# Moving the halves of x by 32 bytes, and adding a three-pass product at the old place

## The reference

```python
def first_block(x, ...):
    for i in range(2):
        h = rmsnorm(x, mix_norm[i])
        x = x + (pool_mixer(h, ...) if i == 0 else chunk_attention(h, ...))
        h = rmsnorm(x, ffn_norm[i])
        x = x + conv_ffn(h, ffn_w_gate[i], ffn_w_val[i], ...)     # D_FF = 2816
    return x

def conv_ffn(h, w_gate, w_val, conv_w, conv_b, w_out):
    a = h @ w_gate                       # then a causal convolution over 3 tokens
    return (jax.nn.silu(a) * (h @ w_val)) @ w_out

def second_block(x, ...):
    proj = rmsnorm_2(x, norm_attn) @ w_in
    # retention, group norm, silu gate            -> y_a = ret @ w_branch_ret
    # stick-breaking attention                    -> y_b = sb @ w_branch_sb
    x = x + (sigmoid(ga) * y_a + sigmoid(gb) * y_b) @ w_out
    x = x + peer(rmsnorm_2(x, norm_ffn), ...)      # 16384 experts, top 16 per head
    return x
```

## Time and profile before

| | |
|---|---|
| Median of 3 runs | 1524.32 us (1523.0 to 1524.53) |
| The profiled execution, its own time | 1520.35 us |
| Its span, from the first instruction to the last | 1518.5 us |
| Instructions | 26337 |
| TensorE matmuls, busy | 1488.9 us, 98% of the span |
| VectorE, ScalarE, GpSimd busy | 1107.8, 764.5, 328.1 us |
| Granted TensorE clock | full, in all 40 slices |
| Read from HBM | 341.92 MB, 226 GB/s over the span |

### The profile page before, as it was taken

How to read it: one execution, slowest core, us unless ns; L and a number is a source line. 1 busy time by engine, 2 the same in 40 slices (tenths; PEclk the granted TensorE clock), 3 DMA queues, 4 the chain that set the end, 5 groups by cost and what they waited for, 6 DMA issues and landing times.

```text
span 1518.5 us, 26337 instructions
## 1 busy us (share of the span) xinstructions
PE 1488.9 (98%) x10162; PEld 1374.1 (90%) x10162; DVE 1107.8 (73%) x2153; ACT 764.5 (50%) x1562; POOL 328.1 (22%) x240
## 2 busy tenths in 40 slices
PE   6999999999999999999999999999999999999998
PEld 6999997799999988899999999999999977777777
DVE  6766678767666776766768895677777688888887
ACT  7555555555555556444454113443343366666665
POOL 1111113202111121001016001233232223332330
PEclk9999999999999999999999999999999999999999
DMA  5666556445656564444544577999999889888885
GB/s 186 190 193 189 189 196 212 132 140 166 186 191 193 170 204 161 144 139 138 172 154 140 169 241 260 335 316 351 322 312 326 320 308 314 302 303 311 307 311 185
DMA packets 95852, 344.68 MB, mean 227 GB/s; under 512 B 10665, under 2 KB 11953, under 8 KB 95729
## 3 DMA queue, kind: packets, MB, share of 16 engines
q1 hardware_dynamic: 77296, 275.89, 55.8%
q0 software_dynamic: 18432, 67.12, 12.2%
HBM read 341.92 MB, written 1.05 MB: 226 GB/s over the span
## 4 chain that ended last, share of the span: by engine, by line
PE 77%; DVE 8%; DMA 7%; ACT 4%; issue 3%; POOL 1%; DVEq 0%; SPq 0%; ACTq 0%; POOLq 0%
PE ps L1008 76%; DMA RAW<-wall 7%; DVE WL L443 2%; ACT WH L612 2%; DVE YS L1543 2%; POOL FS L529 1%; DVE XT L1540 0%; PE ps L1174 0%; DVE GG L1540 0%; DVE SS L1543 0%; DVE SQN L1540 0%; DVE HL L1543 0%; POOL SM L496 0%; ACT SQN L619 0%; ACT HH L630 0%
## 5 line engine op out<-in xcount | busy, mean ns | idle before, releaser
L443 DVE TENSOR_TENSOR WL<-RAW,WH 128x1024 fp32r<-128x1024 f32 x361 | 443.0, 1227 | 184.3 <-ACT WH L612 172.0
L612 ACT ACTIVATE WH<-RAW 128x1024 fp32r<-128x1024 f32 x354 | 372.8, 1055 | 249.0 <-PE ps L1008 233.2
L1008 PE MATMUL ps<-XT,RAW 128*128 128x192 f32 x2048 | 343.9, 327 | 0.1
L1008 PEld LDWEIGHTS ps<-XT,RAW 128*128 128x128 f32 x2048 | 331.5, 190 | 0.3 <-ACT BIG L905 0.3
L1008 PE MATMUL ps<-HH,WH 128*128 128x256 f32 x976 | 277.0, 284 | 0.4 <-DVE WL L443 0.4
L1008 PE MATMUL ps<-HL,WH 128*128 128x256 f32 x976 | 272.7, 279 | 0.0
L1008 PE MATMUL ps<-HH,WL 128*128 128x256 f32 x976 | 272.6, 279 | 0.0
L1008 PE MATMUL ps<-WH,GG 128*128 128x512 f32 x768 | 266.8, 398 | 4.5 <-DVE GG L1540 4.3
L1008 PE MATMUL ps<-WL,GG 128*128 128x512 f32 x512 | 201.7, 394 | 0.0
L1008 PEld LDWEIGHTS ps<-WH,GG 128*128 128x128 f32 x768 | 144.4, 188 | 46.4 <-DVE GG L1540 12.4
L1008 PEld LDWEIGHTS ps<-HH,WH 128*128 128x128 f32 x976 | 183.5, 188 | 3.1 <-issue 2.5
(11 more groups left out here) (271 smaller groups left out, 2442.7 us busy)
## 6 DMA issues: line engine op xcount, KB each, us to landing
RAW<-wall SPq DMA_DIRECT2D x510, 512.0 KB
B<-rel SPq DMA_DIRECT2D x4, 768.0 KB, 5.9
DEC<-con SPq DMA_DIRECT2D x4, 384.0 KB, 4.2
XT<-xt SPq DMA_DIRECT2D x4, 256.0 KB, 4.6
UB<-utab,IDXU POOLq DMA_INDIRECT x64
VB<-wall,IDXV POOLq DMA_INDIRECT x64
WIN<-con SPq DMA_DIRECT2D x1, 768.0 KB, 7.7
out<-XT SPq DMA_DIRECT2D x2, 256.0 KB, 2.6
```

Source lines behind the costliest of these rows:

```text
L443: ins = eng.tensor_tensor(wl, RAW[:, b % NRAW, :], wh.bitcast(F), ALU.subtract)
L612: act.activation(halves(b)[0], RAW[:, b % NRAW, :], ACT.Copy).then_inc(s_hi, 1)
L1008: return pe.matmul(o, l, r, start=start, stop=stop, skip_group_check=True)
```

## The change

EM is allocated ahead of HH and HL instead of behind SQN. A view THIRD is added: of each half of x, 256 columns beginning at column 24, hence 96 bytes into the tile. A function `settle` makes one three-pass product with THIRD as the moving operand and the first 128 columns of the block's weights, and writes it where the block's own first product goes, which then starts its sum anew. `block` and `accumulate` take a flag for it. It is set for val block 2 of each FFN and for the first wout block of the mixers. What is computed stays the same.

```diff
--- before.py
+++ after.py
@@ -270,10 +270,9 @@
 
         early = ExitStack()
         sb("SHIFT", [128, 8], F, early)
+        EM = sb("EM", [128, 2], F, early)
         HH, HL = sb("HH", [128, KD, T], R, early), sb("HL", [128, KD, T], R, early)
         SQN = sb("SQN", [128, KD, T], F, early)
-
-        EM = sb("EM", [128, 2], F, early)
 
         with ExitStack() as sub:
             EH, EL = sb("EH", [128, 2, BLK], R, sub), sb("EL", [128, 2, BLK], R, sub)
@@ -331,6 +330,8 @@
             IDXU, IDXV = sb("IDXU", [128, NSP], U32, ph), sb("IDXV", [128, NSP], U32, ph)
             GS, DOTS, AS = (sb(n, [128, NSP], F, ph) for n in ("GS", "DOTS", "AS"))
             ZERO = sb("ZERO", [128, 64], F, ph)
+
+        THIRD = [x[:, 0:2, :].rearrange("p k t -> p (k t)")[:, 24:24 + T] for x in (HH, HL)]
 
         MROT = GB[:, :, :].rearrange("p k t -> p (k t)").rearrange("p (g t c) -> p g t c", g=2, t=2)
 
@@ -1024,8 +1025,15 @@
                         ins.then_inc(done_k, 1)
                 return ins
 
-            def block(b, o, hi=HH, lo=HL, per_k=None, done_k=None):
+            def settle(b, o):
+
+                wh, wl = halves(b)
+                mm3(o, wh[:, 0:128], wl[:, 0:128], THIRD[0], THIRD[1], True, True)
+
+            def block(b, o, hi=HH, lo=HL, per_k=None, done_k=None, settled=False):
                 wait_low(pe, b)
+                if settled:
+                    settle(b, o)
                 project(b, o, hi, lo, KD, 0, per_k, done_k).then_inc(s_blk, 1)
 
             def direct(b, o):
@@ -1035,9 +1043,11 @@
                     ins = mm(o, RAW[:, b % NRAW, c128(k)], XT[:, k, DENSE], k == 0, k == KD - 1)
                 ins.then_inc(s_blk, 1)
 
-            def accumulate(b, hi, lo, first=False, free=None, at=0):
+            def accumulate(b, hi, lo, first=False, free=None, at=0, settled=False):
 
                 wait_low(pe, b)
+                if settled:
+                    settle(b, acc(0, at))
                 wh, wl = halves(b)
                 for m in range(KD):
                     if free is not None and m % 2 == 0:
@@ -1139,7 +1149,7 @@
                 for j in range(1, JF):
                     if j >= 2:
                         pe.wait_ge(s_v3, base + j - 1)
-                    block(AT[f"val{l}", j], bank[5 + 2 * (j % 2)][:, 0:T])
+                    block(AT[f"val{l}", j], bank[5 + 2 * (j % 2)][:, 0:T], settled=j == 2)
                     if j < JF - 1:
                         pe.wait_ge(s_v0, base + j)
                         block(AT[f"gate{l}", j + 1], bank[4 + 2 * ((j + 1) % 2)][:, 0:T])
@@ -1394,7 +1404,7 @@
                 elif n < 70:
                     m = 5 if n == 69 else (n - 58) // 2
                     pe.wait_ge(s_gl, 2 * JF + m + 1)
-                    accumulate(b, MH[:, m % 3, :], ML[:, m % 3, :], m == 0)
+                    accumulate(b, MH[:, m % 3, :], ML[:, m % 3, :], m == 0, settled=m == 0)
                 else:
                     accumulate_last(b, [(MH[:, m % 3, :], ML[:, m % 3, :]) for m in (6, 7)],
                                     [(s_gl, 2 * JF + 7), (s_gl, 2 * JF + 8)])
```

## The result

The changed kernel is slower. Over 19 runs each, its median is 1526.28 us (1523.88 to 1529.2) against 1522.15 us (1519.28 to 1528.01); the ratio is 1.0028, interval [1.0021, 1.0036], so 4.3 us or 0.28% more, with 3.2 to 5.5 us as its interval. The profiled execution has a span of 1526.6 us against 1518.5.

What follows compares the result with a forecast made beforehand. TensorE's queue was taken as the bound, through the distance between product starts. Terms: -6.32 + 0.15 - 1.13 + 0.5 = -6.8 us, so median 1524.32 - 6.8 = 1517.5; own range 1513.5 to 1520.5, 8 in 10 1512.5 to 1527.

Steps and rivals of the forecast that it cites:

- Part 1: EM ahead of HH: x moves from 32 to 64 modulo 128, no instruction added, nothing for the other engines.
- Part 2: Settle ahead of val 2 in each FFN: three products switch to the fast pace as 48 did; cost +0.72 us.
- Part 3: Rest of each FFN at the fast pace, 113.33 ns: 3.52 us less per FFN, 7.04 for both.
- slower: Rival, chance 0.15: three products don't switch or the fast pace needs x at 32; FFNs +6.1 us, time 1531.4.
- Part 5: Settle ahead of the mixers' last products (wout 0): cost +0.35 us, net -1.13 if fast pace holds, else +0.35.
- Parts 4, 6 and 7: FFN blocks ahead of settling +0.15 us; unsettled x in mixers +0.4, query blocks +0.1; x as stationary operand 0.

Runs made afterwards that it cites:

- runs 15: Changed kernel, THIRD at 160 modulo 256, the mixers' three added matmuls moved from wout 0 to rbr 2: 1513.22 us against 1520.76 before, ratio 0.9949.
- 16: Changed kernel, the mixers' three added matmuls moved from wout 0 to rbr 2, THIRD kept at 32 modulo 256: ratio 1.0034 to the kernel before.
- run 11: Changed kernel with only THIRD moved to 160 modulo 256, measured again with a second profile: ratio 0.9975 to the kernel before.
- runs 13: Changed kernel with four matmuls at 160 modulo 256 in place of each added three: ratio 1.0024 to the kernel before.
- 17: Changed kernel with two matmuls at 160 modulo 256 in place of three, ahead of val 2 and rbr 2: ratio 1.0013 to the kernel before.
- run 3: Changed kernel with only THIRD moved from 32 to 160 modulo 256, first measurement: ratio 0.9984 to the kernel before.
- experiment 5: Changed kernel without added products, FH and FL moved to 160 modulo 256: ratio 0.9986 to the kernel before.
- experiment 4: Changed kernel with 24 matmuls at 160 modulo 256 in place of each added three: ratio 1.0073 to the kernel before.
- experiment 14: Changed kernel with eight matmuls at 160 modulo 256 in place of each added three: ratio 1.003 to the kernel before.

## Why the prediction was wrong

*Part 1, the move of x:* right up to the mixers' end, without a new wait of TensorE and without a slower engine: ScalarE's writes of HH take 506 ns against 507 and VectorE's of HL 481 against 482. The one new wait, 0.8 us for a DMA at 1207.64, lies in the last stages.

*Part 2, the switch:* the step that failed. I wrote that the steps behind slow FH are alike from the second on, "so I take it that three do what 48 did", at a place called "32 modulo 128 as x was before". That is true modulo 128, but x was at 160 modulo 256 and THIRD is at 32. The added steps are 119, 121 and 117 ns in the first FFN of the changed kernel and 118, 118 and 117 in the second, not 117 and then 120 as at 46.74 in the earlier trace rows, and the pairs of runs 15 and 16 show that this place decides. The number was not what failed first: at 160, where the first steps were 117, 120 and 120 as in the kernel before (run 11, first FFN), three did what 48 did. But a number isn't a minimum either, as runs 13 and 17 show.

*Part 3:* the size was right where it applied. The forecast said 149.60 us for the 1320 products with the switch; one FFN of run 3 and both of 11 and 15 have that. For the case without it, the rival "slower" had 1320 x 117.75 = 155.43; the changed kernel has 155.47. The gap of 5.87 us per FFN between the two outcomes hung on one unmeasured transition, and there I gave 0.60 to the side that failed and 0.15 to the one that came.

*Part 5, the mixers:* I took -1.13; what came is the other case, +0.35 (739.64 to 779.71 is 40.07 us against 39.72). The reading "two of three paces lead to fast" was no evidence: behind that wait none of the tries worked.

*Parts 4, 6 and 7:* small, as forecast. Most of the 52 blocks of x as the stationary operand kept their pace; those with weights in EH and EL became faster (last section). Query blocks are at either pace.

*The rival that came true* gave 1531.4 - 1524.32 = +7.1 us; measured are 4.3. Its FFN term was right within 0.05 us per FFN over the long stretch; up to the mixers' end the trace has 5.4 us. The rival had +0.16 for the last 36 products of each FFN; in the first FFN they came out fast behind the wait, and from out 19 to the second FFN's out 1 the trace is 0.57 us shorter (208.07 to 365.10 against 205.30 to 362.90). The rest, of the forecast against the trace and of the trace against the runs, is left open.

*The time by itself:* 1526.28 us lies inside the 1512.5 to 1527 given for 8 chances in 10, and that is no merit. The range was set around 1524.32, the median of three runs, and for a faster kernel; over 19 runs the kernel before has 1522.15, and the change went the other way.

*Lines of 16 bytes:* The Trainium skill, "SBUF — State Buffer", section "Door 1: The DMA port swizzle", says that SBUF has lines of 16 bytes. All places tried here begin such a line, so this doesn't tell them apart, and the runs do: shifts of 32 and of 128 bytes change a matmul's step by up to 6.7 ns (120.0 against 113.3).

*What the steps show, read afterwards:* with the starts in ns, as the traces have them, the number of matmuls at 160 and their first steps together tell the outcome of every try that comes out of the slow pace inside an unbroken run, without an exception in these profiles:
- A first step of 114 or 115 (and a second, where there is one, of 120 or 121): a single matmul switches (4 of 4) and three do (8 of 8); two, four and eight don't (0 of 2, 1 and 2), nor do the blocks of 24 in the first FFN of experiment 5.
- First steps of 116, 116, 115: neither three, four nor 24 switch (0 of 1, 1 and 2).
- A first step of 116 or 117 and a second of 120: two, three, 24 and 48 switch (1 of 1, 2 of 2, 1 of 1 and 2 of 2); a single matmul with 117 doesn't (0 of 8).

So 24 isn't too many by itself: a block of 24 at 160 did switch in experiment 5, second FFN, and the 24 of experiment 4 both came in with 116, 116, 115. This was found by sorting results, not forecast and tested, and some groups have one try.

*Open:* what sets the first step, and why nothing at 32 modulo 256 switched. The start times have a memory that they don't show themselves: in experiment 14 the added matmuls fall into the same steps 113, 116, 118, 120 as x in the kernel before, yet 117.7 follows, where before 113.3 did. What in TensorE or in its reading of SBUF holds that state was not found.

## What to carry to other kernels

Where TensorE is never idle and its products still differ in pace, compare start times by operand and note the operands' addresses modulo 256; here that was worth 0.5% in one direction and 0.6% in the other (x at 96). A state that is carried from product to product can't be inferred from a transition of another length or place: when the two outcomes of one transition lie on both sides of the present time, price both and split the chance evenly until the exact transition is measured. What switches such a state should stand in an unbroken run, once, and be checked in a profile of each stage and in many runs: the same code switched in one execution and not in another (the third kernel and the eleventh).

## What the runs showed that I had not expected

- One shape, several paces by the place of the moving operand, for 128x256 float32r products at full clock: 113.3 and 117.7 to 117.8 at 192 modulo 256; 116.7 (as steps of 113, 116, 118, 120) and 120.0 at 160; a pattern of 114 to 120 at 32. An FFN of 1320 such products takes 149.60, 152.80 or 155.47 us, the same within 0.01 in each profile that takes that way.
- The 113.3 pace lasts: 1320 products without anything at 32. It ended at a wait of TensorE (experiment 15: 113.3 up to 206.29, 117.8 behind 207.53) or with a few matmuls at 160 modulo 256. A wait can also start it, as at 213.08 in the changed kernel.
- The same two paces exist for 512 columns. The first two blocks behind an FFN have their weights in EH and EL, at 64 modulo 128, and there the weights are the moving operand: in the changed kernel the 19 steps from 218.43 to 222.74 are 226.8 ns, twice 113.4, where the blocks with weights at 0 have 233.2. The place of the weights isn't all of it: in the kernel before, with x as the stationary operand at 32, the same two blocks took 214.69 to 220.29, 233.3 ns each, and with x at 96 they are at 233.1. The two lines marked L1008 are from the kernel before:

```profile
214.69 0.40 PE L1008 MATMUL ps<-EH,HH 128*128 128x512 f32 x1
...
220.29 0.40 PE L1008 MATMUL ps<-WH,HH 128*128 128x512 f32 x1
...
218.43 0.39 PE L1009 MATMUL ps<-EH,HL 128*128 128x512 f32 x1
...
222.74 0.39 PE L1009 MATMUL ps<-WH,HH 128*128 128x512 f32 x1
```
